# A gated delta rule whose token inverse is taken in 64x64 chunks, in a two-layer diffusion trunk on one core

## The chip, the core and the metric

The kernel runs on one core of one Trainium2 chip. The metric is the device time of one execution in microseconds. TensorE is called PE in the rows (PEld for its weight loads), VectorE DVE, ScalarE ACT, GpSimd POOL, and SyncE, which issues most loads, SP.

## What is computed

Two layers of a trunk over two samples of 128 tokens (prompt and latent), model width 1024. Each layer: modulated norm, one input projection, four groups of heads side by side (gated delta rule, retention, neighbourhood attention, short convolution; 4 heads of 64 each), output projection, and then 32 experts, top 2 of one group. The modulation ("ada") is a product of the conditioning with a 1024 x 6144 matrix, in 8 tiles of 768 columns. Everything is float32. What the change is about is the delta rule, run forwards and on the flipped tokens:

```python
decay = jnp.exp(jnp.where(causal, gc[..., :, None] - gc[..., None, :], -jnp.inf))
kb = k * bt[..., None]
low = jnp.where(strict, jnp.einsum('nbhcd,nbhed->nbhce', kb, k) * decay, 0.0)
t_inv = lax.linalg.triangular_solve(eye + low, jnp.broadcast_to(eye, low.shape), left_side=True, lower=True)
u = t_inv @ (v * bt[..., None])
w = t_inv @ (kb * jnp.exp(gc)[..., None])
attn = jnp.einsum('nbhcd,nbhed->nbhce', q, k) * decay
def step(s, xs):
    qd, at, ui, wi, kd, cd = xs
    v_new = ui - wi @ s
    o = qd @ s + at @ v_new
    s = s * cd[..., None, None] + jnp.einsum('bhcd,bhce->bhde', kd, v_new)
    return s, o
```

The reference takes chunks of 64 tokens; the result does not depend on the size of the chunk.

## The kernel before

Each engine has its own program, written out by hand, and the engines wait for one another by named semaphores (`sem[...]`; `rise(l, name, n)` is the count to wait for in layer l). On TensorE, VectorE, ACT and GpSimd the two layers are one loop (`Fori(0, DEPTH)`, L398, L882, L1136, L1570), so the counts to wait for are computed in registers, and the end of the body branches back. SyncE's program has its two layers written out. At the end of a layer the experts' part stands twice, once for the case that no expert has over 32 tokens, which is the one taken, and once for the other (`pe.If`, `pe.Else`, L802 and L841).

Weights come through a ring of four slots of 3 MB. A load waits until the product that last used its slot is done: 8 ada tiles, 5 pieces of the input projection, 3 of the output projection, 32 experts. The first expert's load waits for ada tile 7, the next three for the pieces of the output projection.

Order of a layer on TensorE: ada tiles 0 to 2 (L414) and the norm's sums (L430); input projection (L454 to L480); attention and retention (L487 to L564), with ada tiles 3 and 4 in between; the delta rule (L569 to L694); output projection (L708); router (L720); experts (L743 gathers tokens, L769 gate and up, L783 down, L792 scatters).

The delta rule treats a sample of 128 tokens as one chunk. For sample s (first 0, then 1) TensorE makes the gates' differences (L578, L579), the products of keys with keys and queries (L586), beta along the rows (L592) and some small ones, VectorE masks and multiplies (L1347 to L1359). Then the inverse of the 128x128 unit triangular matrix of each of 4 heads and 2 directions g is built by doubling, in 7 levels b:

```python
for h in range(HEADS):
    last = mm(ps[:, 2 + g, h * P:(h + 1) * P], group(g, 6)[:, h, :],
              group(g, 3)[:, h, :] if b else ident, start=True, stop=True)   # L633
for h in range(HEADS):
    last = mm(ps[:, 4 + g, h * P:(h + 1) * P], group(g, 4)[:, h, :], group(g, 5)[:, h, :], start=True, stop=True)  # L654
for h in range(HEADS):
    last = mm(ps[:, g, h * P:(h + 1) * P], group(g, 5)[:, h, :], group(g, 4)[:, h, :], start=True, stop=True)      # L658
```

`group(g, 6)` is the level's part of the triangle (GpSimd, L1631), `group(g, 3)` and `group(g, 4)` the inverse so far and its transpose (VectorE adds to them, L1397 and L1399), `group(g, 5)` the first product copied out by ACT (L1046). Level 0 has only L633, level 6 lacks L654. Ada tiles 5 and 6 are cut into pieces between the levels of sample 0, tile 7 stands at the start of sample 1. Then come the products with the values (L671), outputs (L683), for sample 0 the states (L689). After both samples the outputs are normed (ACT L1050, PE L694, ACT L1053 and L1055, DVE L1419 and L1421).

Each float32 product is two instructions in the trace, two loads and two matmuls. Where a product has a `tile_position`, it uses a part of the array: the ada products and gate and up use four tiles of all rows and 32 columns (128*32), the scatter four tiles of 32 rows (32*128).

## Time and profile before

| | us |
|---|---|
| median of 3 runs | 1213.41 (1213.16 to 1215.55) |
| profiled execution, its own time | 1213.35 |
| its span | 1211.7 |
| mean granted TensorE clock | 0.922 of full |

| layer 0, us from the span's start | stage |
|---|---|
| 0 to 42 | ada tiles 0 to 2, first norm |
| 42 to 137 | input projection |
| 137 to 181 | attention, retention |
| 181 to 313 | delta rule |
| 313 to 369 | output projection, second norm, router |
| 369 to 606 | experts |

Layer 1 begins behind 606 and takes the same stages. The span counts from the first to the last instruction of the profiled execution. A busy engine is not an engine that sets the time: what counts is which wait ends last in a stage. "Issue" in a row is time in which an engine waited for nothing that the profile shows.

### The profile page before, as it was taken

The page shows a single profiled execution, that of the slowest core. Times are in us where ns is not written, and L with a number is a line of the kernel's source. Part 1 is how long each engine was busy: PE and PEld are TensorE (multiplying, and loading weights), DVE is VectorE, ACT ScalarE, POOL GpSimd, SP SyncE. Part 2 cuts the span into 40 slices and gives each one's busy share as a digit, 9 for nine tenths or more (in the row PEclk, how much of TensorE's full clock was granted, in tenths as well). Part 3 has the DMA queues.
Part 4 walks back from the last instruction along what each step waited for, and adds up shares of the span by engine and source line. Part 5 has one row for each costly group of instructions (what it writes and reads, how often), then busy time and mean ns, then how long its engine had stood idle before and what let it go on. Part 6 is the DMA issues. An engine that isn't in the chain of part 4 may idle for free.

```text
span 1211.7 us, 28903 instructions
## 1 busy us (share of the span) xinstructions
PE 995.8 (82%) x12852; PEld 828.6 (68%) x12852; DVE 345.9 (29%) x701; ACT 259.3 (21%) x566; POOL 86.6 (7%) x93
## 2 busy tenths in 40 slices
PE   4889868989878897787757998699899698878775
PEld 3489767879766665555544996588888676666653
DVE  0155644354133000000023546443541510000001
ACT  1224431202012111111113353211120221111111
POOL 0000112213000000000000002022320000000000
PEclk9789988999978999999877999799999699999998
DMA  9944631021162999999987355111203459999993
GB/s 387 428 176 170 271 121 39 4 92 51 39 274 111 429 424 430 429 427 428 426 342 294 145 207 219 74 36 36 110 2 148 164 231 426 426 429 428 428 425 167
DMA packets 15668, 299.69 MB, mean 247 GB/s; under 512 B 2224, under 2 KB 2224, under 8 KB 2736
## 3 DMA queue, kind: packets, MB, share of 16 engines
q1 hardware_dynamic: 15120, 296.67, 58.9%
q8 instruction: 108, 1.77, 0.6%
q0 software_dynamic: 416, 1.05, 0.3%
q14 instruction: 24, 0.20, 0.0%
HBM read 295.61 MB, written 2.10 MB: 246 GB/s over the span
## 4 chain that ended last, share of the span: by engine, by line
PE 58%; DMA 24%; issue 7%; DVE 6%; ACT 3%; POOL 1%; SPq 0%; DVEq 0%; POOLq 0%; ACTq 0%
DMA ring<-in_moe 22%; PE ps L769 6%; PE ps L708 5%; PE ps L478 4%; PE ps L633 4%; PE ps L479 4%; PE ps L480 4%; PE ps L658 4%; PE ps L654 3%; PE ps L783 3%; PE ps L454 3%; PE ps L743 3%; DMA ring<-in_ada_w 2%; PE ps L414 2%; PE ps L792 2%
## 5 line engine op out<-in xcount | busy, mean ns | idle before, releaser
L769 PE MATMUL ps<-ring,arena 128*32 128x128 f32 x4096 | 136.1, 285 | 73.4 <-DMA ring<-in_moe 62.4
L769 PEld LDWEIGHTS ps<-ring,arena 128*32 128x32 f32 x4096 | 115.2, 114 | 101.3 <-DMA ring<-in_moe 57.8
L478 PE MATMUL ps<-arena_r 128*128 128x256 f32 x384 | 109.9, 286 | 10.4 <-DVE ring_r L1198 10.4
L1540 DVE COPY arena<-ps 128x128 f32<-128x128 f32 x64 | 18.7, 292 | 339.8 <-PE ps L769 339.8
L480 PE MATMUL ps<-arena_r,ring_r 128*128 128x256 f32 x384 | 108.9, 284 | 0.0
L479 PE MATMUL ps<-hT_r,arena_r 128*128 128x256 f32 x384 | 108.7, 283 | 0.0
L1098 ACT ACTIVATE arena<-ps 128x256 f32<-128x256 f32 x64 | 24.6, 384 | 298.4 <-PE ps L783 298.4
L414 PE MATMUL ps<-ring,condp 128*32 128x128 f32 x1536 | 58.3, 303 | 31.1 <-DMA ring<-in_ada_w 15.4
L478 PEld LDWEIGHTS ps<-arena_r 128*128 128x128 f32 x384 | 73.7, 192 | 10.6 <-DVE ring_r L1198 10.6
L743 PE MATMUL ps<-arena 128*128 128x128 f32 x512 | 75.3, 294 | 3.2 <-DVE arena L1520 3.2
L783 PE MATMUL ps<-ring,arena 128*32 128x256 f32 x1024 | 72.6, 386 | 3.8 <-issue 3.8
L743 PEld LDWEIGHTS ps<-arena 128*128 128x128 f32 x512 | 64.2, 198 | 14.5 <-issue 11.1
L792 PE MATMUL ps<-arena 32*128 32x256 f32 x1024 | 73.3, 400 | 1.0 <-ACT arena L1098 1.0
L479 PEld LDWEIGHTS ps<-hT_r,arena_r 128*128 128x128 f32 x384 | 73.7, 192 | 0.0
L480 PEld LDWEIGHTS ps<-arena_r,ring_r 128*128 128x128 f32 x384 | 73.6, 192 | 0.0
L414 PEld LDWEIGHTS ps<-ring,condp 128*32 128x32 f32 x1536 | 46.5, 122 | 39.0 <-issue 23.8
L1198 DVE TENSOR_TENSOR ring_r<-ring,arena_r 128x2048 fp32r<-128x2048 f32 x24 | 54.8, 2291 | 56.7 <-ACT arena_r L936 56.4
L1631 POOL TENSOR_TENSOR arena<-arena,const 128x512 f32<-128x512 f32 x56 | 60.5, 1094 | 125.5 <-PE ps L633 65.0
L708 PE MATMUL ps<-hT,ring 128*128 128x256 f32 x256 | 59.5, 396 | 5.7 <-DVE hT L1421 5.7
L708 PEld LDWEIGHTS ps<-hT,ring 128*128 128x128 f32 x256 | 50.8, 199 | 14.9 <-DVE hT L1421 7.4
L633 PE MATMUL ps<-arena 128*128 128x128 f32 x384 | 51.8, 290 | 5.9 <-POOL arena L1631 5.8
L633 PEld LDWEIGHTS ps<-arena 128*128 128x128 f32 x384 | 47.9, 202 | 9.3 <-DVE arena L1391 5.2
(278 smaller groups left out, 1357.0 us busy)
## 6 DMA issues: line engine op xcount, KB each, us to landing
ring<-in_moe SPq DMA_DIRECT2D x64, 3072.0 KB, 18.1
ring<-in_ada_w SPq DMA_DIRECT2D x16, 3072.0 KB, 11.4
ring<-in_w_feat SPq DMA_DIRECT2D x8, 3072.0 KB, 17.6
ring<-in_w_tok SPq DMA_DIRECT2D x2, 2112.0 KB, 27.5
ring<-in_w_out SPq DMA_DIRECT2D x2, 2048.0 KB, 7.1
ring<-in_w_out SPq DMA_DIRECT2D x4, 1024.0 KB, 4.8
param<-in_param SPq DMA_DIRECT2D x2, 1442.0 KB, 23.2
xT<-in_xT SPq DMA_DIRECT2D x1, 1024.0 KB, 12.5
```

The source lines that it names most:

```text
L414: last = mm(ps[j:j + 32, bank_in, 0:P], condp[:, k, lead:lead + 32], slot[:, k * 768 + m * P:k * 768 + (m + 1) * P], start=u < 4, stop=u > ...
L478: mm(out, hi, ph_hi[:, k, :], start=k == 0, stop=False)
L479: mm(out, hi, h_lo[:, k, :], start=False, stop=False)
L480: last = mm(out, low[:, k, tile], ph_hi[:, k, :], start=False, stop=k == KT - 1)
L633: last = mm(ps[:, 2 + g, h * P:(h + 1) * P], group(g, 6)[:, h, :], group(g, 3)[:, h, :] if b else ident, start=True, stop=True)
L708: last = mm(ps[:, f // 2, (f % 2) * TOK:(f % 2 + 1) * TOK], slot[:, at:at + P], hT[:, k, :], start=k == 0, stop=k == KT - 1)
L743: last = mm(ps[:, gather_bank(q, k // 2), 256 + (k % 2) * P:256 + (k % 2 + 1) * P], ht[:, s, k * P:(k + 1) * P], sel[:, s, QUAD * q:QUAD * ...
L769: last = mm(ps[32 * j:32 * j + 32, 4, 0:P], xg[:, e // QUAD % 2, k, cols], slot[:, at:at + P], start=k == 0, stop=k == KT - 1, tile_positi ...
L783: last = mm(ps[32 * j:32 * j + 32, 6, 0:256], act_t[:, e % 2, kk * CAP:(kk + 1) * CAP], slot[:, at:at + 256], start=kk == 0, stop=kk == 1, ...
L792: last = mm(ps[:, j, half * TOK:(half + 1) * TOK], ye[rows, e % 2, half * P:(half + 1) * P], spread[rows, e % 2, :], start=False, stop=e = ...
L1198: tt(tiles768(ring_r[in_load(i) % RING][:], cols), tiles768(ring[in_load(i) % RING][:], cols), pw_hi[v % 2], ALU.subtract).then_inc(sem["p ...
L1631: G.tensor_tensor(group(g, 6), group(g, 2), bc(levels[:, g, b, :].unsqueeze(1), HEADS, P), ALU.mult)\
```

## The change

The delta rule's matrices are cut into 64-token chunks, and both samples go together. A group g is now a sample and a direction (4 groups), and holds for 4 heads two 64x64 blocks, one per half of the partitions. `by_chunk` makes 8 products, 4 heads in each of the tiles (0, 0) and (64, 64). The doubling has 6 levels instead of 7, each over 4 groups, `against(n)` (the first product) running two steps ahead of `onto(n)` (the two that extend the inverse and its transpose; in the last level only the transpose). In place of level 6, the values are solved in three thin rounds: the first chunk's, what crosses into the second chunk, and the second chunk's. The gates' differences are made from a row product and a per-partition scalar, with 16 masks on VectorE and the products moved ahead of the retention's variance; keys are multiplied by beta before the key products. Ada tile 5 stands ahead of the key products, tile 6 between the thin rounds, tile 7 behind the states, each whole. The padded copies of keys and queries (POOL L1585 and L1595, ACT L993) and the zeroing of L1614 and L1615 go. The constants get three new blocks (320 columns, ahead of the levels' masks), and the masks shrink. The layer loop is written out on all engines.

```diff
-LEVELS = 7
+LEVELS = 6
+CHUNK = 64
...
+    ("neg_f", P), ("neg_b", P), ("eye", CHUNK),
+    ("levels", 2 * LEVELS * CHUNK))
...
-            with pe.Fori(0, DEPTH) as l:
+            for l in range(DEPTH):
...
+                for g in range(4):
+                    s, d = divmod(g, 2)
+                    for h in range(HEADS):
+                        last = mm(ps[:, 4 + g, h * P:(h + 1) * P], bc(gdec[:, s, d * 4 + h:d * 4 + h + 1], P), upto[d], start=True, stop=True)
+                    last.then_inc(sem["gr_mm"], 1)
...
+                                n, at = d * 4 + 2 * j + i, (2 * j + s) * P
+                                last = mm(ps[part64(i), d, at:at + P], bc(beta[:, s, n:n + 1], CHUNK), ident, start=True, stop=True,
+                                          tile_position=(0, CHUNK * i), skip_group_check=True)
+                    last.then_inc(sem["brow_mm"], 1)
...
+                pe.wait_ge(sem["kd_dve"], rise(l, "kd_dve", 1))
+                ada(ADA_FIRST + 2, 2)
...
+                def by_chunk(out, weights, moving):
+                    for h in range(HEADS):
+                        for c in range(2):
+                            last = mm(out[part64(c), h * CHUNK:(h + 1) * CHUNK], weights[part64(c), h, :], moving(c, h),
+                                      start=True, stop=True, tile_position=(CHUNK * c, CHUNK * c), skip_group_check=True)
+                    return last
...
+                    by_chunk(ps[:, 4 + g % 2, 0:256], low_b[:, g],
+                             (lambda c, h: inv[part64(c), g, h, :]) if b else (lambda c, h: ident[part64(c), part64(c)])).then_inc(sem["inv_dmm"], 1)
...
+                    if b < LEVELS - 1:
+                        by_chunk(ps[:, 2 + g % 2, 0:256], inv_t[:, g], lambda c, h: prod[part64(c), g, h, :])
+                    by_chunk(ps[:, 2 + g % 2, 256:512], prod[:, g], lambda c, h: inv_t[part64(c), g, h, :]).then_inc(sem["inv_umm"], 1)
...
+                for n in range(4 * LEVELS + 2):
+                    if n < 4 * LEVELS:
+                        against(n)
+                    if n > 5:
+                        onto(n - 2)
...
+                    pe.wait_ge(sem["inv_upd"], rise(l, "inv_upd", step(LEVELS - 1, g)))
+                    for h in range(HEADS):
+                        last = mm(ps[part64(c), solve_bank(g), h * CHUNK:(h + 1) * CHUNK], inv_t[part64(c), g, h, :], z[part64(c), g, h, :],
+                                  start=True, stop=True, tile_position=(CHUNK * c, CHUNK * c), skip_group_check=True)
+                    last.then_inc(sem["first_mm"], 1)
+                pe.wait_ge(sem["at_dve"], rise(l, "at_dve", 1))
...
+                pe.wait_ge(sem["off_dve"], rise(l, "off_dve", 1))
...
+                        last = mm(ps[part64(1 - c), solve_bank(g), h * CHUNK:(h + 1) * CHUNK], off[part64(c), s, h, :], vn[part64(c), g, h, :],
+                                  start=True, stop=True, tile_position=(CHUNK * c, CHUNK * (1 - c)), skip_group_check=True)
+                    last.then_inc(sem["cross_mm"], 1)
...
+                ada_transpose(ADA_FIRST + 3, 7)
...
+                last.then_inc(sem["gs_mm"], 1)
+                ada(ADA_FIRST + 4, 6)
...
-            with act.Fori(0, DEPTH) as l:
+            for l in range(DEPTH):
...
+                        act.wait_ge(sem["inv_dmm"], rise(l, "inv_dmm", 4 * b + g + 1))
+                        go(prod[:, g].rearrange("p h c -> p (h c)"), ps[:, 4 + g % 2, 0:256], ACT.Copy).then_inc(sem["inv_dev"], 1)
...
-            with dve.Fori(0, DEPTH) as l:
+            for l in range(DEPTH):
...
+                    for h in range(HEADS):
+                        last = stt(decay[:, g, h, :], ps[:, 4 + g, h * P:(h + 1) * P], ngc[:, 4 * g + h:4 * g + h + 1], neg[g % 2], ALU.add, ALU.add)
+                    last.then_inc(sem["gr_mask"], 1)
...
+                    last = tt(kb[:, d].rearrange("p j s t -> p (j s t)"), A("qkv")[:, 512:1024], bank(d), ALU.mult)
+                last.then_inc(sem["kb_dve"], 1)
...
+                        last = tt(four(low[part64(c), g]), kk, four(decay[part64(c), g, :, part64(c)]), ALU.mult)
...
+                    tt(inv[:, g], ps[:, 4 + g % 2, 0:256].rearrange("p (h c) -> p h c", h=HEADS), eye, ALU.add)
+                    tt(inv_t[:, g], low_b[:, g], eye, ALU.add).then_inc(sem["inv_upd"], 1)
...
+                            t = both[:, g].rearrange("p b h c -> p (b h c)")
+                            tt(t, t, bank(2 + g % 2), ALU.add).then_inc(sem["inv_upd"], 1)
+                        else:
+                            t = inv_t[:, g].rearrange("p h c -> p (h c)")
+                            tt(t, t, ps[:, 2 + g % 2, 256:512], ALU.add).then_inc(sem["inv_upd"], 1)
+                        if b == 1:
+                            last = value(g)
+                            if g % 2 == 1:
...
-            with pool.Fori(0, DEPTH) as l:
+            for l in range(DEPTH):
...
+                        G.tensor_tensor(low_b[:, g], low[:, g], bc(levels[:, g % 2, b, :].unsqueeze(1), HEADS, CHUNK), ALU.mult)\
+                         .then_inc(sem["inv_c"], 1)
```

TensorE in one level of the inverse (ps is PSUM, arena the work space in SBUF). Before, one of two groups:

```order
L627 REGISTER_ALU
L629 REGISTER_ALU [waits inv_c]
L633 MATMUL ps<-arena 128x128 [waits inv_upd]
L633 MATMUL ps<-arena 128x128 x3
...
L650 REGISTER_ALU
L651 REGISTER_ALU [waits inv_dev]
L654 MATMUL ps<-arena 128x128 [waits inv_upd]
L654 MATMUL ps<-arena 128x128 x3
L658 MATMUL ps<-arena 128x128 x4
```

Now, one and a half of four groups, of the steps `against` (8 products) and `onto` (16):

```order
L634 MATMUL ps<-arena 64x64 [waits inv_dev,inv_upd,inv_c]
L634 MATMUL ps<-arena 64x64 x7
L634 MATMUL ps<-arena 64x64 [waits inv_dev,inv_upd]
L634 MATMUL ps<-arena 64x64 x15
L634 MATMUL ps<-arena 64x64 [waits inv_dev,inv_upd,inv_c]
```

The products keep their number per group and shrink from 128x128 to 64x64; the register instructions are gone, the waits stand on the products.

TensorE behind the inverse. Before, for a sample:

```order
L671 MATMUL ps<-arena 128x64 [waits inv_upd]
L671 MATMUL ps<-arena 128x64 x3
L683 MATMUL ps<-arena 128x128 [waits ada_dve,vn_dve]
L683 MATMUL ps<-arena 128x128 x7
L689 MATMUL ps<-arena 128x256 [waits kd_dve]
```

Now, for both samples:

```order
L684 MATMUL ps<-arena 64x64 x3
L404 MATMUL ps<-ring,condp 32x128 [waits slot_in3,at_dve]
L404 MATMUL ps<-ring,condp 32x128 x47
L694 MATMUL ps<-arena 64x64 [waits first_act,off_dve]
...
L412 MATMUL ps<-const,adarow 128x12 [waits ada_row,const_in]
L702 MATMUL ps<-arena 64x64 [waits rest_dve]
...
L714 MATMUL ps<-arena 64x128 [waits qd_dve,vn_dve]
...
L721 MATMUL ps<-arena 64x64 x8
L404 MATMUL ps<-ring,condp 32x128 [waits slot_in0]
L404 MATMUL ps<-ring,condp 32x128 x47
L727 MATMUL ps<-arena,const 128x512 [waits ada_dve,gn_sq]
```

Three thin rounds (L684, L694, L702) with ada tile 6 between, then outputs, states, and ada tile 7 ahead of the norm's product (L727).

TensorE at the end of a layer, the last rows of the case that is not taken (its loop L868, now L901). Before:

```order
L868 COMPARE_AND_BRANCH
L841 UNCONDITIONAL_BRANCH
L398 REGISTER_ALU
L398 COMPARE_AND_BRANCH
L147 UNCONDITIONAL_BRANCH
```

Now, the end of layer 0:

```order
L901 COMPARE_AND_BRANCH
L874 UNCONDITIONAL_BRANCH
L404 MATMUL ps<-ring,condp 32x128 [waits slot_in0,layer_done,cond_silu]
L404 MATMUL ps<-ring,condp 32x128 x47
L419 MATMUL ps<-arena,const 128x256 [waits norm_sq]
```

The branch back at L398 is gone, and layer 1's first ada products stand behind the unused case.

## Rows read from the trace of the kernel before

**Rows 1.** The page: engines' busy time; DMA queue: packets, MB, share
```profile
PE 995.8 (82%) x12852; PEld 828.6 (68%) x12852; DVE 345.9 (29%) x701; ACT 259.3 (21%) x566; POOL 86.6 (7%) x93
q1 hardware_dynamic: 15120, 296.67, 58.9%
```

**Rows 2.** Windows: us, busy PE, PEld, DVE, ACT, POOL, PEclk, DMA share, GB/s
```profile
200.00:240.00 40.00, 38.79 (x383) 35.00 (x384) 19.60 (x30) 6.51 (x12) 14.07 (x13) 0.96 0.08 28
...
345.00:369.00 24.00, 14.33 (x65) 13.07 (x63) 11.67 (x51) 6.98 (x17) 0.00 (x0) 0.63 0.38 150
...
445.00:606.00 161.00, 128.18 (x2586) 95.19 (x2582) 11.08 (x43) 24.75 (x85) 0.00 (x0) 0.97 1.00 427
```

**Rows 3.** The chain of waits: start us, us, what; both layers
```profile
181.44 1.14 PE ps L564 x2
...
309.15 1.14 PE ps L694 x2
...
313.13 22.67 PE ps L708 x96
...
778.97 1.14 PE ps L564 x2
...
910.52 22.67 PE ps L708 x96
```

**Rows 4.** Timeline, one level: start us, us, engine, operation [idle before]
```profile
282.22 1.95 PE L633 MATMUL ps<-arena 128*128 128x128 f32 x16
...
283.32 0.60 ACT L1046 ACTIVATE arena<-ps 128x512 f32<-128x512 f32 x1 [4.00 <-PE ps L633]
...
284.04 1.15 PE L654 MATMUL ps<-arena 128*128 128x128 f32 x8
...
285.23 0.69 DVE L1397 TENSOR_TENSOR arena<-arena,ps 128x512 f32<-128x512 f32 x1 [2.12 <-PE ps L654]
...
287.71 1.95 PE L633 MATMUL ps<-arena 128*128 128x128 f32 x16
```

**Rows 5.** Timeline, products in tiles and thin products
```profile
155.98 2.83 PE L414 MATMUL ps<-ring,condp 128*32 128x128 f32 x96
...
302.44 2.00 PE L671 MATMUL ps<-arena 128*128 128x64 f32 x16
...
374.64 1.96 PE L769 MATMUL ps<-ring,arena 128*32 128x128 f32 x64 [0.55 <-ACT arena L1074]
...
604.06 1.15 PE L792 MATMUL ps<-arena 32*128 32x256 f32 x16 [0.50 <-ACT arena L1098]
```

**Rows 6.** Timeline and page, single costs of the other engines
```profile
265.08 0.42 DVE L1371 TENSOR_TENSOR arena<-ps,egc 128x256 f32<-128x256 f32 x1
...
606.05 4.22 DVE L1428 SCALAR_TENSOR_TENSOR xT<-ps,adaT,xT 128x128 f32<-128x128 f32 x16 [4.58 <-PE ps L792]
...
L1631 POOL TENSOR_TENSOR arena<-arena,const 128x512 f32<-128x512 f32 x56 | 60.5, 1094 | 125.5 <-PE ps L633 65.0
```

**Rows 7.** L398's branch; timeline between the layers; DMA issues of 590:625 us
```profile
L398 PEldq COMPARE_BRANCH  x2: 79/3764/7450, 611.2 to 1205.1; - x2
...
610.30 0.33 SPq L370 DMA_DIRECT2D param<-in_param  x1
...
619.01 5.33 PE L414 MATMUL ps<-ring,condp 128*32 128x128 f32 x93 [13.81 <-issue]
...
629.64 2.29 DVE L1155 TENSOR_TENSOR hT<-xT,rstd 128x2048 f32<-128x2048 f32 x1 [19.36 <-ACT rstd L902]
...
636.17 3.19 ACT L910 ACTIVATE hT<-hT,adaT,scale 128x128 f32<-128x128 f32 x8 [0.90 <-DVE scale L1148]
...
param<-in_param SPq DMA_DIRECT2D x1, 59.5 KB, 16.1
```

**Rows 8.** Timeline: the start, the experts' loads
```profile
32.20 5.26 PE L414 MATMUL ps<-ring,condp 128*32 128x128 f32 x96 [3.55 <-DMA ring<-in_ada_w]
...
267.23 77.57 SPq L328 DMA_DIRECT2D ring<-in_moe  x4
```

591 lines of the change are left out of this document (284 added, 307 removed).

## The prediction

> **What bounds the kernel now.** The page comes first: TensorE is busy for 82% of the span, VectorE for 29%, and the DMA engines for 59% [rows 1]. An average hides where each of them ends the waits, so the windows come next. While the experts' weights stream in, the DMA share is 1.00 at 427 GB/s; in the delta rule (200 to 240 us) it is 0.08 and TensorE is busy for 38.8 of 40 us [rows 2]. The kernel is a chain of stages in which TensorE is the limit, then a stage in which the DMA is, once per layer. The change works in the first kind only.
>
> Then the chain of waits gives the length of what changes. From the retention's variance product (L564) to the first product of the output projection (L708) it takes 313.13 - 181.44 = 131.7 us in layer 0 and 910.52 - 778.97 = 131.6 us in layer 1 [rows 3]. This is over a fifth of the span, twice 131.7 = 263 us. The timeline of one doubling level of the second sample shows what it is made of: L633 starts at 282.22 and again at 287.71, 5.49 us later, and between them stand 48 instructions of 128x128 (L633 x16, then L654 and L658, x8 each, for either group), that is 0.112 us each [rows 4]. ACT (0.60 us) and VectorE (0.69) lie beside it. Counting all levels of both samples, a layer has 72 such groups of 8, 64 us of TensorE.
>
> **The inverse, now.** It has 6 levels, and 4 groups (two samples, two directions) follow one another. A helper, by_chunk, issues 8 products of 64x64, each as 2 instructions: 16 instructions. Calls per layer: 24 in against(), 2 in each of the 16 onto() of the levels 1 to 4, 1 in each of the last 4, together 60 calls in place of the 72 groups. So the price of one call decides. No row shows a product in a 64x64 tile. The nearest rows: four tiles of 128x32 (the ada products) stream 96 instructions in 2.83 us, 0.029 each; and weights of the full width against 64 columns (L671) cost 2.00 / 16 = 0.125 each, the same as wide ones [rows 5]. Half of the columns should load in half the time, 0.056 in place of 0.112, and a call alternates between two tiles on different rows; that loads on different rows overlap is seen in L792 (four tiles of 32 rows, each with weights 128 wide: 1.15 / 16 = 0.072 [rows 5], though a load of that width takes 35.00 / 384 = 0.091 [rows 2]). The bounds are 0.029 and 0.125. I take 0.033, near the first, because its rows are tiled as these are, and a little above it for the two or three waits ahead of each call. A call is 16 x 0.033 = 0.53 us, 60 calls 31.8 us.
>
> Does anything else bound a step? A step (one group of one level) is 3 calls, 1.6 us. VectorE adds 128x512 in 0.69 and then does one piece of other work: 0.42 for 128x256 [rows 6], at most three of these (1.3) for the second sample's values. ACT copies 128x256, half of the 128x512 that take 0.60 [rows 4], and GpSimd multiplies 128x256, half of the 128x512 that take 1.09 [rows 6]. All but those two steps fit; the groups' latencies are covered by the other groups. I add 3.0 us for level 0, where only two groups fit in PSUM and two adds (0.8 us) stand between them. **Inverse: 34.8 us.**
>
> **Before it**, from the moment L564 starts now (its input is ready): VectorE has 16 mask instructions of 128x128, at 4.22 / 16 = 0.26 us together 4.2 us [rows 6]. TensorE does what is left of the gate products (32 instructions from L561's end on, 2.1 us of them still to come), then the variance product (1.1); ACT follows with a logarithm and an exponential (1.25), VectorE with the retention's last two instructions (1.4). They end at 5.9 us. Two 128x256 and two 128x512 follow (kdg, kb): 8.0 us. TensorE meanwhile goes on: ada tile group 5 (2.83 us) runs from 6.6 to 9.4, the key products by chunk 32 instructions x 0.04 = 1.3, and then what needs no answer: 32 + 16 + 8 + 16 instructions and a transpose, some 4.1 us. With the hand-overs **15.3 us** to the first inverse product; VectorE's 8 multiplications of 64x256 (3.0) end inside this.
>
> **After it**: three rounds of thin products (first solve, crossing, second solve), each 32 instructions that stay in one tile for 8 at a time, at half of L633's price, 0.055: 1.8 us each; ada group 6 between the first two (2.83); an answer of ACT or VectorE behind each (0.4 to 0.6); then the outputs (48 x 0.055 = 2.65), copy and square (1.4), ada group 7 (2.83), the norm's product (1.1), two ACT and two VectorE instructions (2.7), as between 309.15 and 313.13 now [rows 3]. With the hand-overs **19.7 us**. Of the ada work nothing is saved: it now stands in the chain, 3 x 2.83 us, but it did before too, in pieces.
>
> Sum: 15.3 + 34.8 + 19.7 = 69.8 us instead of 131.7: 61.9 us less per layer, 123.8 in all.
>
> Here a rule speaks against a term. All loads of L654 are on the same rows as the products before them, and yet 8 of them take 0.112 us each, with 0.11 needed by the product alone [rows 4]: load and product overlap. The Trainium skill, page "TensorE: Matmul & The Clock Gate", Part 3, states that a weight load overlaps products in flight only when their row groups differ. By that rule the 12 groups of thin products would take twice 0.44 us, 5.3 us more per layer, and the sum would end near 1095; the trace disagrees, and I keep 0.055.
>
> **The layer loop.** TensorE's last expert product of layer 0 starts at 604.06 and its next one at 619.01; it sits idle for 13.81 us with no releaser. The loop's line shows why: its branch back starts at 611.2 and takes 7450 ns [rows 7], and the engine had come past the unused case by then, 6 us after its last product. VectorE ends the layer at 610.27 [rows 6]. Written out, the way past the unused branch of the experts stays (until 611.2), the branch back goes: a start 7.7 us earlier. What is late next is the small parameter load: issued at 610.30, 16.1 us to landing, 626.4; VectorE waits for it ahead of L1155, which starts at 629.64 now [rows 7]. Behind it (2.3 us) the last ada columns follow, two rounds of TensorE, VectorE and ACT at some 2.0 us: the modulation starts at 630.7 instead of 636.17, **5.5 us** earlier; the ends are 0 (the next code is fetched as slowly) and 7.7. At the start 320 more columns of constants go ahead of the third ada load, for which TensorE waits at 32.20 [rows 8]: 0.16 MB at 427 GB/s, **+0.4 us**. Register instructions vanish from the queues; where an engine waits anyway they cost nothing, and I count nothing.
>
> **Later stages.** The first expert's load was issued at 267.23 [rows 8] since ada group 7 was early; now it goes some 6 us ahead of the output projection. At 427 GB/s its 3 MB take 7.4 us, and gate and up products of expert 0 start at 374.64 [rows 5], 61 us behind the projection's start: hidden. The other loads hang on the projection and on the experts as before, so the DMA-bound stage keeps its length.
>
> Forecast: the profiled execution took 1213.35 us (span 1211.7), within 0.1 us of the median; 1213.35 - 123.8 - 5.5 + 0.4 = **1084.5 us**.
>
> **Rivals.**
> 1. *Two tiles in turn, not together.* If a call's two tiles do not overlap, an instruction costs 0.055, a call 0.88, the inverse 60 x 0.36 = 21 us more per layer: 1127. Against it: L792 and the ada rows overlap fully. For it: L792's row tiles write four different PSUM banks, by_chunk's two write the same one. The page "TensorEngine Tiling (Array Packing)" of the Trainium skill, Restrictions and Gotchas, states that different row tiles cannot access the same PSUM bank simultaneously; no row here shows such a pair. Chance 0.16.
> 2. *A step waits for answers.* If hand-overs are not covered and a step takes 2.1 us, 20 steps give 10 us more per layer: 1105. Chance 0.13.
> 3. *TensorE's clock.* The granted clock is 0.63 from 345 to 369 us, where TensorE pauses, and 0.96 in the levels [rows 2]. If small tiles count for little and it stays at 1.2 GHz in the inverse, that doubles 32 us per layer: 1148. Against it: 0.97 among the experts' tiles [rows 2]. Chance 0.05.
> 4. *Slower than before.* If an instruction in a 64x64 tile costs what L671's does, 0.125, a call is 2.0 us, the inverse 123 us, the 96 instructions of the thin rounds 7 us dearer, and a layer 15.3 + 123 + 19.7 + 7 = 165 us, 33 more than 131.7: 1213 + 66 - 5 = 1274. It decides from about 0.10 us on: (131.7 + 2.5 - 38) / 960. Chance 0.03.
>
> The forecast itself has 0.60; 0.03 is left for less than the range. The low end is instructions at 0.029 (3.8 us less per layer), 7.7 at the loop and 4 us less per layer elsewhere: 1067. The high end takes in rival 1 with nothing gained at the loop: 1134. A measurement of this kernel tells 0.2%, 2.4 us, from no change. Faster 0.96, within it 0.01, slower 0.03.
>
> **What would show it.** L634: 960 instructions per layer, 16 in some 0.5 us, 35 us from first to last; the chain from L567 to L741 near 70 us; idle before L404 in layer 1 under 7 us, and L1185 waiting for the parameters. I am wrong if L634's x16 take 0.9 us or more, if "issue" ahead of them adds up to over 5 us, or if the experts' stage grows.

## The result, and the profile after

| | before | changed |
|---|---|---|
| median of the runs | 1214.35 us (4 runs, 1213.16 to 1215.55) | 1074.99 us (4 runs, 1072.14 to 1077.56) |
| profiled execution, its own time | 1213.35 | 1072.84 |
| its span | 1211.7 | 1070.9 |
| mean granted TensorE clock | 0.922 | 0.930 |

The ratio is 0.8843, with a 95% interval of 0.8812 to 0.8874. The forecast was 1084.5 us. The changed kernel is 9.5 us faster than that by the medians and 11.7 us by the profiled executions, and lies inside the range of 1067 to 1134.

The page of the changed kernel, the engines' busy time and the DMA queue, answers to [rows 1]:

```profile
PE 880.6 (82%) x13868; PEld 730.0 (68%) x13868; DVE 306.6 (29%) x685; ACT 246.5 (23%) x562; POOL 48.5 (5%) x77
...
q1 hardware_dynamic: 15120, 296.31, 66.6%
```

TensorE has 115 us less to do, with 1016 instructions more, and its share is 82% as before. The gain lies in what a product costs, not in how many there are.

The windows in the delta rule and among the experts (columns as in [rows 2]):

```profile
200.00:240.00 40.00, 38.13 (x1142) 36.81 (x1144) 24.94 (x49) 9.46 (x25) 11.54 (x18) 1.00 0.09 30
...
386.00:547.00 161.00, 121.56 (x2448) 91.36 (x2452) 14.54 (x56) 25.60 (x79) 2.00 (x3) 0.95 1.00 427
```

From 200 to 240 us TensorE issues 1142 instructions where it issued 383, at a granted clock of 1.00. The experts' stretch runs at a DMA share of 1.00 and 427 GB/s in both kernels. From the first product of the output projection to the end of the layer on VectorE it takes 543.8 - 247.2 = 296.6 us now and 610.27 - 313.13 = 297.1 before: that stage has kept its length.

The chain of waits through the delta rule of layer 0 (start us, us, what), which answers to [rows 3]:

```profile
184.17 0.88 PE ps L567 x2
188.49 2.83 PE ps L404 x96
...
192.35 0.46 PE ps L605 x32
...
196.34 0.64 PE ps L634 x16
...
228.77 1.32 PE ps L684 x32
230.09 2.76 PE ps L404 x96
...
247.19 20.99 PE ps L741 x96
```

and its marks in layer 1:

```profile
706.49 0.88 PE ps L567 x2
...
718.67 0.64 PE ps L634 x16
...
750.65 1.32 PE ps L684 x32
```

The variance product is now L567. VectorE's masks (L1368) start when its input is ready, at 182.0 and 704.3 us; this is the point from which the prediction counts. From there to the output projection (L741, at 247.19 and 769.08) it takes 65.2 and 64.8 us, in place of 131.7 and 131.6.

TensorE's timeline has the durations (start us, us, line, shapes, count, [idle before]):

```profile
191.25 1.10 PE L596 MATMUL ps<-arena 64*64 64x128 f32 x32
192.17 0.64 PE L605 MATMUL ps<-arena 64*64 64x64 f32 x32
...
201.00 9.53 PE L634 MATMUL ps<-arena 64*64 64x64 f32 x304 [0.32 <-DVE arena L1429]
210.77 18.00 PE L634 MATMUL ps<-arena 64*64 64x64 f32 x576 [0.24 <-POOL arena L1671]
228.61 1.49 PE L684 MATMUL ps<-arena 64*64 64x64 f32 x32
```

and its windows have the price of an instruction where nothing interrupts the stream (instructions of L634 alone: us, busy PE, PEld, granted clock, DMA share, GB/s):

```profile
217.00:224.00 7.00, 7.00 (x242) 7.00 (x244) 1.00 0.02 5
```

The 576 instructions from 210.77 take 18.00 us, 0.0313 each. Between 217 and 224 us the price is 7.00 / 242 = 0.029; the rest of the 18.00 us is in a few short breaks, the longest 0.34 us, in which no instruction starts. L596 and L605 use four tiles of 64x64: 32 instructions of 128 columns in 1.10 us, and 32 of 64 columns in 0.64. Such a duration ends with the last instruction's own time (0.22 us for L605), which weighs on a short group; in the chain, which goes on with the next product, L605 has 0.46 us, 0.014 each.

Between the layers, the timeline of all engines, which answers to [rows 7]:

```profile
539.57 4.23 DVE L1487 SCALAR_TENSOR_TENSOR xT<-ps,adaT,xT 128x128 f32<-128x128 f32 x16 [4.56 <-PE ps L825]
543.82 0.33 SPq L364 DMA_DIRECT2D param<-in_param  x1
...
545.62 4.91 PE L404 MATMUL ps<-ring,condp 128*32 128x128 f32 x92 [6.88 <-issue]
...
558.27 2.29 DVE L1185 TENSOR_TENSOR hT<-xT,rstd 128x2048 f32<-128x2048 f32 x1 [14.48 <-DMA param<-in_param]
...
562.71 3.18 ACT L943 ACTIVATE hT<-hT,adaT,scale 128x128 f32<-128x128 f32 x8 [0.96 <-DVE scale L1178]
```

The idle time ahead of layer 1's first ada tile is 6.88 us of issue, in place of 13.81. The modulation starts 562.71 - 543.80 = 18.9 us behind layer 0's end; before, it was 636.17 - 610.27 = 25.9.

Where the 140.8 us of span went, from these marks:

| stretch | before | changed | less |
|---|---|---|---|
| start to the output projection, layer 0 | 313.13 | 247.19 | 65.9 |
| to the end of layer 0 (VectorE) | 297.1 | 296.6 | 0.5 |
| to the modulation of layer 1 | 25.9 | 18.9 | 7.0 |
| to the output projection, layer 1 | 274.35 | 206.37 | 68.0 |
| to the end | 301.2 | 301.8 | -0.6 |

### The profile page after: what moved, and what is told of

Read it like the earlier page. It is cut to its first block, busy times and chain, and to the rows that moved or that the text cites. A ratio compares the mean times of both kernels' runs of the same rounds, so it can differ in the third digit from the quotient of the medians.

```text
span 1070.9 us, 30181 instructions
## 1 busy us (share of the span) xinstructions
PE 880.6 (82%) x13868; PEld 730.0 (68%) x13868; DVE 306.6 (29%) x685; ACT 246.5 (23%) x562; POOL 48.5 (5%) x77
## 4 chain that ended last, share of the span: by engine, by line
PE 55%; DMA 31%; DVE 7%; ACT 3%; issue 2%; SPq 0%; POOL 0%; DVEq 0%; POOLq 0%; ACTq 0%
DMA ring<-in_moe 29%; PE ps L802 6%; PE ps L741 5%; PE ps L634 5%; PE ps L467 4%; PE ps L469 4%; PE ps L468 4%; PE ps L404 3%; PE ps L443 3%; PE ps L816 3%; DMA ring<-in_ada_w 3%; PE ps L776 2%; PE ps L825 2%; PE ps L753 1%; DVE xT L1487 1%
## 5 line engine op out<-in xcount | busy, mean ns | idle before, releaser
L802 PE MATMUL ps<-ring,arena 128*32 128x128 f32 x4096 | 133.9, 286 | 77.2 <-DMA ring<-in_moe 76.2
L1599 DVE COPY arena<-ps 128x128 f32<-128x128 f32 x64 | 18.6, 291 | 346.7 <-PE ps L802 346.7
L467 PEld LDWEIGHTS ps<-arena_r 128*128 128x128 f32 x384 | 73.7, 192 | 10.7 <-issue 10.7
L776 PE MATMUL ps<-arena 128*128 128x128 f32 x512 | 76.1, 296 | 3.3 <-DVE arena L1579 3.3
L776 PEld LDWEIGHTS ps<-arena 128*128 128x128 f32 x512 | 65.1, 201 | 15.7 <-issue 15.7
L404 PE MATMUL ps<-ring,condp 128*32 128x128 f32 x1536 | 52.7, 300 | 24.9 <-DMA ring<-in_ada_w 15.8
L816 PE MATMUL ps<-ring,arena 128*32 128x256 f32 x1024 | 69.8, 390 | 0.0
L404 PEld LDWEIGHTS ps<-ring,condp 128*32 128x32 f32 x1536 | 47.9, 121 | 28.6 <-issue 25.9
L741 PE MATMUL ps<-hT,ring 128*128 128x256 f32 x256 | 59.1, 394 | 5.5 <-DVE hT L1480 5.5
L741 PEld LDWEIGHTS ps<-hT,ring 128*128 128x128 f32 x256 | 50.6, 198 | 13.1 <-DVE hT L1480 5.7
L634 PE MATMUL ps<-arena 64*64 64x64 f32 x1792 | 55.6, 219 | 2.1 <-DVE arena L1429 1.3
L634 PEld LDWEIGHTS ps<-arena 64*64 64x64 f32 x1792 | 53.9, 135 | 3.8 <-POOL arena L1671 2.4
L825 PEld LDWEIGHTS ps<-arena 32*128 32x128 f32 x1024 | 46.5, 184 | 11.5 <-ACT arena L1128 2.0
```

The source lines that it names most:

```text
L404: last = mm(ps[j:j + 32, bank_in, at:at + P], condp[:, k, lead:lead + 32], slot[:, k * 768 + m * P:k * 768 + (m + 1) * P], start=u < 4, st ...
L467: mm(out, hi, ph_hi[:, k, :], start=k == 0, stop=False)
L634: last = mm(out[part64(c), h * CHUNK:(h + 1) * CHUNK], weights[part64(c), h, :], moving(c, h), start=True, stop=True, tile_position=(CHUNK ...
L741: last = mm(ps[:, f // 2, (f % 2) * TOK:(f % 2 + 1) * TOK], slot[:, at:at + P], hT[:, k, :], start=k == 0, stop=k == KT - 1)
L776: last = mm(ps[:, gather_bank(q, k // 2), 256 + (k % 2) * P:256 + (k % 2 + 1) * P], ht[:, s, k * P:(k + 1) * P], sel[:, s, QUAD * q:QUAD * ...
L802: last = mm(ps[32 * j:32 * j + 32, 4, 0:P], xg[:, e // QUAD % 2, k, cols], slot[:, at:at + P], start=k == 0, stop=k == KT - 1, tile_positi ...
```

## The experiments

Times are medians; the kernel before took 1214.0 to 1214.8 us in the three sets of runs.

### 1. The layer loop alone

The kernel before, and on each of the four engines:

```diff
-            with pe.Fori(0, DEPTH) as l:
+            for l in range(DEPTH):
```

> The kernel before, with the layer loop written out on the four engines and nothing else changed. The prediction's term for this is 5.5 us less, 1213.4 - 5.5 = 1207.9 us, with the branch of 7450 ns gone between the layers and the modulation 5.5 us earlier behind the end of layer 0, and the rest of the kernel as long as before. In the changed kernel the stretch from layer 0's end to the modulation is 7.0 us shorter (18.9 in place of 25.9). Theory A: that is all due to the loop, so this kernel takes 1206 to 1207 us and shows the same 18.9 us. Rival B: part of the 7.0 us comes from elsewhere, and this kernel gains 4 us or less. Rival C: register instructions ahead of products cost time too, then it gains over 9 us, and the stretch from L564 to L708 shrinks below 131 us.

Measured: 1206.43 us (1205.12 to 1208.1), ratio 0.9933 (0.9913 to 0.9952), 8 us less by the medians and 7.0 by the spans. Its timeline between the layers:

```profile
605.95 4.22 DVE L1428 SCALAR_TENSOR_TENSOR xT<-ps,adaT,xT 128x128 f32<-128x128 f32 x16 [4.21 <-PE ps L792]
...
611.71 3.90 PE L414 MATMUL ps<-ring,condp 128*32 128x128 f32 x82 [6.23 <-issue]
...
631.31 3.18 ACT L910 ACTIVATE hT<-hT,adaT,scale 128x128 f32<-128x128 f32 x8 [0.96 <-DVE scale L1148]
```

Layer 0 ends at 605.95 + 4.22 = 610.17, and the modulation (ACT, L910) starts at 631.31, 21.1 us later, in place of 25.9. The idle time ahead of L414 has fallen to 6.23 us. So 4.8 us lie where the prediction had put 5.5, and the changed kernel has another 2.2 us there. Some of this is scatter between executions: VectorE's wait for the small parameter load lasts 15.35 us here and 14.48 in the first profile of the changed kernel, but 15.33 in its second (run 9), where the modulation starts 19.5 us behind layer 0. Within its first ada tile the changed kernel waits 0.63 us for instructions, this one 2.35, between 82 and 14 of them; what sets such a wait was not tried. Another 1.7 us come up to L564 of layer 1, which starts at 772.43 in place of 778.97: the input projection's first products take 15.70 and 3.64 us (L454, L459) where they took 16.67 and 4.51, at a granted clock of 0.88 in place of 0.76 over the 14 us from the start of the modulation. Whether the shorter wait between the layers gave this clock back no run shows: the changed kernel waits hardly longer and has 0.76 there.

In the delta rule the chain is as long as before, from L564 at 181.98 to L708 at 313.42, 131.4 us: the register instructions ahead of the wide products cost nothing. So theory A is right in the total, and has 4.8 of its 7.0 us in the stretch that it named; rivals B and C fall.

### 2. The order of the two tiles

```diff
                 def by_chunk(out, weights, moving):
-                    for h in range(HEADS):
-                        for c in range(2):
+                    for c in range(2):
+                        for h in range(HEADS):
```

> The changed kernel, with the two loops of by_chunk exchanged: the four products of one 64x64 tile, then the four of the other. Nothing else differs. Theory A (the two tiles run beside each other only when a product of one stands directly behind one of the other): an instruction costs what it does in the thin rounds, whose 32 in one tile at a time take 1.49 us, 0.047 each, in place of 0.031. A call then takes 0.75 us instead of 0.50, the 60 calls 15 us more per layer, and the kernel 30 us more: 1105 us. Rival B (one tile after the other, as the prediction's rival 1 has it, 0.055): 23 us per layer, 1121 us. Rival C (the order does not matter, since queued products of both tiles overlap, or VectorE and not TensorE sets the step): within 5 us of the changed kernel's 1075.

Measured: 1088.61 us (1086.39 to 1089.7). The chain, inverse of layer 0:

```profile
201.44 31.51 PE ps L634 x864
```

An instruction costs 31.51 / 864 = 0.0365 us in place of 0.0313. The inverse, from its first product to the first thin solve, takes 37.1 us in both layers in place of 32.3 and 31.9, 10.0 us more in all; the other 3 to 4 us of the medians are not in this stretch. None of the three theories had the size. The two tiles do work beside each other, and best when their products alternate; but with four of one tile in a row most of the overlap is still there.

The traces of the single instructions say why theory A's price was off. In the changed kernel's first thin round (L684) instructions that follow one another in one tile start 0.058 us apart (228.61, 228.66, 228.72, 228.78, 228.84). Where the tile changes, instructions of the two tiles start in pairs, 0.004 to 0.006 us apart, one pair every 0.058 us. One tile alone costs 0.058, and two beside each other half of that, 0.029. The 0.047 that theory A took for the price of one tile alone, 1.49 / 32, is neither: the round has stretches of both kinds, and its 1.49 us end with the 0.22 us that the last instruction takes by itself (from first to last start it is 1.27 us, 0.041 each). In this run 16 instructions (8 in one tile, 8 in the other) take 16 x 0.0365 = 0.58 us, ten times 0.058: six of these ten starts are pairs.

### 3 and 4. The price of a call, and the PSUM bank

Ahead of the first products of the last two levels:

```diff
+                    if b > 3:
+                        pe.wait_ge(sem["off_dve"], rise(l, "off_dve", 1))
+                        for _ in range(5):
+                            for h in range(HEADS):
+                                for c in range(2):
+                                    mm(ps[part64(c), 0, h * CHUNK:(h + 1) * CHUNK], low_b[part64(c), g, h, :], inv[part64(c), g, h, :],
+                                       start=True, stop=True, tile_position=(CHUNK * c, CHUNK * c), skip_group_check=True)
```

> The changed kernel with 5 further calls of 16 instructions ahead of each of the 8 first products of the last two levels, 640 instructions per layer, both tiles writing the same PSUM bank (0), whose content is not used. It prices a call by itself. Theory A (TensorE sets the pace of the inverse, 0.031 us per instruction): 20.0 us per layer, 40 us in all, 1115 us. Rival B (the step waits for answers of VectorE and ACT, busy for 24 of its 32 us): the further work is partly hidden in those steps, 30 us or less.

The fourth is the same with `ps[part64(c), c, ...]`: each tile has its own bank.

> As the one with 5 further calls per first product of the last two levels, but the two tiles write different PSUM banks (0 and 1) in place of the same one. The page "TensorEngine Tiling (Array Packing)" of the Trainium skill, Restrictions and Gotchas, states that different row tiles cannot access the same bank simultaneously. Theory A (the bank makes no difference; two tiles on different rows and different partitions overlap either way): the same time as with one bank, within 2 us, 0.031 us per instruction. Rival B (sharing the bank costs something): split banks are cheaper, at best 0.0265 per instruction (half of the 0.053 that the thin rounds suggest for a tile by itself), 6 us less in all.

Measured: 1111.93 us (1110.91 to 1113.98) with one bank, 1111.05 (1106.54 to 1113.94) with two. The chain, one group of the further products (L657) in either; one bank:

```profile
226.23 2.27 PE ps L657 x78
```

two banks:

```profile
231.43 2.27 PE ps L657 x78
```

78 instructions take 2.27 us in both, 0.0291 each. The 1280 further instructions make 1280 x 0.0291 = 37.3 us, and the kernel with one bank is 36.9 us above the changed one: nothing of them is hidden. So TensorE sets the pace of the last two levels, and here it makes no difference whether two tiles on different rows write the same bank or two. The page "TensorEngine Tiling (Array Packing)" of the Trainium skill, Restrictions and Gotchas, says that different row tiles cannot access one bank simultaneously; the traces disagree for two tiles that write different partitions of it, since with one bank too an instruction costs 0.0291 us, half of the 0.058 of one tile alone. Two row tiles on the same partitions of a bank were not tried.

### 5. Half of the inverse's products

```diff
                 def by_chunk(out, weights, moving):
-                    for h in range(HEADS):
+                    for h in range(HEADS // 2):
```

> The changed kernel with by_chunk making the products of two heads in place of four, so half of the inverse's products are left out (and its result for two heads is not the inverse); ACT, VectorE and GpSimd work as before. It shows what stands right behind TensorE in the inverse. Theory A (TensorE alone sets it and the others are well covered): 480 of 960 instructions go, 15 us less per layer, the inverse from 32.3 to 17.3 us, the kernel at 1045 us. Rival B (VectorE is next: 24 of the 32.3 us busy, and a wait of an add for the products of its own step): the inverse stops at 24 to 26 us, 7 us less per layer, the kernel at 1061. Rival C (it was answers all along that set the step): no change, 1075.

Measured: 1066.94 us (1063.45 to 1070.41), 8 us less. From L634's first instruction to the thin solve (196.09 to 223.54 in the chain) layer 0's inverse takes 27.5 us in place of 32.4: a third of the 15 us that the left out work took. The timeline of two steps shows the next limit:

```profile
214.90 0.69 DVE L1421 TENSOR_TENSOR arena<-ps,arena 128x512 f32<-128x512 f32 x1
215.09 0.92 PE L634 MATMUL ps<-arena 64*64 64x64 f32 x24 [0.28 <-POOL arena L1671]
215.50 0.68 DVE L1440 TENSOR_TENSOR arena<-arena,ps 128x512 f32<-128x512 f32 x1
216.09 0.69 DVE L1421 TENSOR_TENSOR arena<-ps,arena 128x512 f32<-128x512 f32 x1
...
216.28 0.92 PE L634 MATMUL ps<-arena 64*64 64x64 f32 x24 [0.28 <-POOL arena L1671]
```

and over four such steps (columns as in [rows 2]):

```profile
214.30:219.00 4.70, 3.63 (x100) 3.20 (x98) 4.70 (x9) 1.53 (x4) 2.54 (x4) 1.00 0.01 3
```

VectorE's two instructions of a step (L1440, the add, and L1421, the scores) stand one behind the other, 1.20 us a step, and TensorE's 24 instructions (0.92 us) wait. The rows put TensorE's wait down to GpSimd (L1671), whose product ends last before it; but each such product is wanted only four steps later, and GpSimd is busy for 2.54 of the 4.70 us, VectorE for all 4.70. With all heads a step has 48 instructions, at 0.029 to 0.0313 us each 1.40 to 1.50 us. So TensorE stands 0.2 to 0.3 us per step above VectorE in the steps in which VectorE has its second instruction, and rival B is right in kind; its 24 to 26 us were a little low. The prediction's second rival (a step of 2.1 us) is excluded.

### 6. The thin rounds in alternating tiles

In each of the three rounds, here the first:

```diff
-                for g in range(4):
-                    s, c = divmod(g, 2)
+                for s in range(NS):
...
-                    pe.wait_ge(sem["inv_upd"], rise(l, "inv_upd", step(LEVELS - 1, g)))
+                    pe.wait_ge(sem["inv_upd"], rise(l, "inv_upd", step(LEVELS - 1, 2 * s + 1)))
                     for h in range(HEADS):
+                        for c in range(2):
+                            g = 2 * s + c
```

> The changed kernel with the three thin rounds in pairs of groups: a product of one tile directly followed by one of the other, as in by_chunk, in place of four in one tile. The waits of a pair then stand ahead of its first product. Theory A: a round's 32 instructions take 32 x 0.031 = 1.0 us instead of 1.49, but the answers start later (a pair ends 0.5 us in, its two answers run one behind the other), so of the 1.5 us per layer at most 1.0 shows: 1 to 2 us less, 1073 to 1074. Rival B (a round is bound by its hand-overs, not by its products): no change within 0.5 us, or slower by up to 1 us.

Measured: 1075.0 us (1067.82 to 1077.97), the changed kernel's time. Its timeline:

```profile
228.34 0.63 PE L684 MATMUL ps<-arena 64*64 64x64 f32 x16
229.19 0.68 PE L684 MATMUL ps<-arena 64*64 64x64 f32 x16 [0.22 <-DVE arena L1448]
...
233.17 1.15 PE L696 MATMUL ps<-arena 64*64 64x64 f32 x32
...
237.59 1.53 PE L719 MATMUL ps<-arena 128*64 128x128 f32 x24 [1.21 <-DVE arena L1475]
```

The second round (L696) has shrunk to 1.15 us from 1.54. The first is split by a wait, and the outputs (L719) start 9.25 us behind the first solve in place of 237.22 - 228.61 = 8.61. What the products give, the hand-overs take back: rival B. (Its ratio is 0.8834, 0.8807 to 0.8862; the changed kernel's is 0.8843.)

### 7 and 8. Ada tile 5 out of the chain

```diff
                 ada(ADA_FIRST + 1, 3)
+                ada(ADA_FIRST + 2, 3, 128)
+                ada_transpose(ADA_FIRST + 1, 4)
...
                 pe.wait_ge(sem["kd_dve"], rise(l, "kd_dve", 1))
-                ada(ADA_FIRST + 2, 2)
```

with its copies on ACT and VectorE moved to match.

> The changed kernel with ada tile 5 moved from the chain ahead of the key products to just behind ada tile 4, into the 5.4 us in which TensorE waits for the attention's VectorE and ACT work ahead of L520; its load was issued early enough. Theory A (the prediction's reading that each ada tile in the delta rule stands in the chain with its 2.83 us, and that the wait ahead of L520 does not depend on it): 2.8 us less per layer, 5.6 in all, 1069.5. Rival B (VectorE's masks, kdg and kb set the moment at which the key products start, and the tile only fills that wait): they could start at 189.5 in place of 191.3, 1.5 us less per layer or nothing, 1072 to 1075.

The eighth kernel adds the sixth's edit.

> The changed kernel with ada tile 5 early and the thin rounds in alternating tiles together. If both gains are real and lie in different waits they add: 5.6 + 1.5 = 7 us less, 1068. If VectorE sets the start of the key products and the thin rounds are bound by hand-overs: 0 to 3 us less.

Measured: 1068.0 us (1064.3 to 1069.11), ratio 0.8788 (0.8766 to 0.8809), and with both 1071.72 (1066.65 to 1073.48), ratio 0.8808 (0.878 to 0.8835). The timeline of tile 5 early, where the key products (L597) start:

```profile
185.00 1.27 DVE L1385 TENSOR_TENSOR arena<-arena,ps 128x512 f32<-128x512 f32 x2
186.33 1.10 PE L597 MATMUL ps<-arena 64*64 64x128 f32 x32 [1.96 <-DVE arena L1385]
```

They start 186.33 - 180.65 = 5.7 us behind the variance product, in place of 191.25 - 184.00 = 7.25. So of the tile's 2.83 us the move is worth 1.6 per layer, and then TensorE waits 1.96 us for VectorE's multiplication by beta (L1385): rival B as to the place. Yet the kernel gained some 7 us and not 3. The rest lies ahead of L571: from the attention's L522 to L571 it takes 14.98 us in layer 0, where the changed kernel has 184.00 - 166.15 = 17.85; in layer 1 it takes 17.39, where the changed kernel has 17.78. Twice 1.6, 2.9 and 0.4 make 6.5 us. That led to the next two.

The two edits together are not faster than tile 5 alone, and with overlapping intervals the two kernels can't be told apart. Nothing speaks for the sum of 7 us from two gains; the thin rounds gave nothing in run 6 either.

### 9 and 10. The wait ahead of L520, and the clock

> The changed kernel itself, so that the next two stand against it on the same chip: 1072 to 1077 us, as in the runs of the result. Its profile tells how far the stretch behind the delta rule (L741, 96 instructions, 20.99 us in layer 0 and 24.00 in layer 1 of the first profile) moves with TensorE's granted clock alone.

The tenth issues ada tile 4's products twice, and nothing moves:

```diff
-                    for u in range(ADA_UNITS):
+                    for u in [u for _ in range(times) for u in range(ADA_UNITS)]:
...
-                ada(ADA_FIRST + 1, 3)
+                ada(ADA_FIRST + 1, 3, times=2)
```

> The changed kernel with the products of ada tile 4 issued twice, the second time over the first with the same values: 96 instructions more per layer in the 5.4 us in which TensorE waits ahead of L520, nothing else moved. In the profile of the changed kernel the clock is at half from 166 to 174 us, behind that wait; with ada tile 5 in it, it stayed at full in layer 0 and fell for 7 us later in layer 1. Theory A (the wait itself costs the clock, and work in it holds the clock up): L520's 12 instructions take 1.5 us in place of 2.83, L533's 24 some 3 in place of 4.8, 1.3 to 3 us less per layer, 2.6 to 6 us less in all, though work is added. Rival B (what ada tile 5 gained came from its move alone): the same time as the changed kernel, with L520 at 2.8 us.

Measured: the changed kernel 1075.22 us (1072.76 to 1076.41), ratio 0.8856 (0.8833 to 0.888); with the tile issued twice 1069.68 (1066.89 to 1071.04), ratio 0.8805 (0.878 to 0.883). With 192 instructions more it is 5.5 us faster. TensorE's timeline of the changed kernel again, layer 0:

```profile
157.99 2.83 PE L404 MATMUL ps<-ring,condp 128*32 128x128 f32 x96
166.24 2.82 PE L520 MATMUL ps<-const,arena 128*128 128x128 f32 x12 [5.42 <-DVE arena L1325]
...
170.60 2.07 PE L533 MATMUL ps<-arena 128*128 128x128 f32 x8 [1.30 <-ACT arena L1049]
```

and of the tenth kernel, layer 1:

```profile
681.98 5.45 PE L404 MATMUL ps<-ring,condp 128*32 128x128 f32 x192
690.23 1.53 PE L520 MATMUL ps<-const,arena 128*128 128x128 f32 x12 [2.81 <-DVE arena L1325]
...
693.30 1.16 PE L533 MATMUL ps<-arena 128*128 128x128 f32 x8 [1.41 <-ACT arena L1049]
```

but in its layer 0:

```profile
165.22 1.56 PE L520 MATMUL ps<-const,arena 128*128 128x128 f32 x12 [2.81 <-DVE arena L1325]
...
168.32 2.07 PE L533 MATMUL ps<-arena 128*128 128x128 f32 x8 [1.30 <-ACT arena L1049]
```

with its windows (the number behind POOL's count is the granted clock), of layer 0 and of layer 1:

```profile
168.00:173.00 5.00, 4.68 (x22) 4.68 (x23) 1.79 (x5) 0.27 (x1) 0.00 (x0) 0.50 0.16 69
690.00:704.00 14.00, 12.36 (x96) 11.58 (x97) 8.65 (x20) 2.05 (x2) 0.56 (x1) 1.00 0.30 126
```

L520's 12 instructions take 1.53 and 1.56 us behind a wait of 2.81, and 2.82 behind one of 5.42. This is no accident of one execution: in all seven traces that keep the long wait (5.20 to 5.43 us; the changed kernel twice and runs 2 to 6) they take 2.82 us in both layers. The changed kernel's windows behind that wait, and of two starts of the output projection (the first profile):

```profile
166.00:174.00 8.00, 6.54 (x30) 6.44 (x31) 4.73 (x10) 1.45 (x1) 0.00 (x0) 0.50 0.16 66
247.00:252.00 5.00, 4.80 (x22) 4.26 (x23) 0.14 (x1) 0.00 (x0) 0.00 (x0) 1.00 0.98 421
769.00:774.00 5.00, 4.92 (x12) 3.94 (x13) 0.02 (x1) 0.00 (x0) 0.00 (x0) 0.50 0.94 403
```

The clock is granted at 0.50 (the 1.2 GHz level) for the 8 us behind the long wait. With the wait half filled it held through layer 1's stretch (690.23 to 704.92, 14.7 us for L520 to L567 in place of 17.8) and fell later in layer 0's (168 to 173 us, 17.1 us). So the fill is worth up to 3 us a layer, not each time: in layer 0 the stretch is 0.7 us shorter, and behind the inverse the clock fell again (0.61 from 234 to 238 us), so that L714's 48 instructions take 4.49 us in place of 2.84 and layer 0 keeps nothing. The two profiled executions differ by 2.9 us in span, the medians by 5.5; where the other 2.6 us lie no trace shows. Theory A holds for what stands right behind the wait (L520 in both layers, its 1.3 to 3 us in layer 1); its sum of 2.6 to 6 us fits the medians. Rival B is excluded, since nothing was moved here. The Trainium skill, page "TensorE: Matmul & The Clock Gate", Part 1, says that the clock has two levels and that an idle stretch brings the lower one back; these rows agree. The second profile also gives what run 9 was for: L741's 96 instructions take 22.41 us in layer 0 and 24.02 in layer 1, where the first profile has 20.99 and 24.00.

### 11. All three ada tiles

Tile 6 follows tile 5 into the wait ahead of L520, and tile 7 is cut into three:

```diff
+                ada(ADA_FIRST + 3, 3, 256)
...
-                ada(ADA_FIRST + 3, 6)
+                ada(ADA_FIRST + 4, 6, units=range(0, 16))
...
-                ada(ADA_FIRST + 4, 6)
+                ada(ADA_FIRST + 4, 6, units=range(16, 32))
                 pe.wait_ge(sem["gn_sq"], rise(l, "gn_sq", 1))
                 mm(bank(7), C("blockones"), gn_a, start=True, stop=True).then_inc(sem["gn_mm"], 1)
+                ada(ADA_FIRST + 4, 6, units=range(32, ADA_UNITS))
```

> The changed kernel with ada tiles 5 and 6 both in the wait ahead of L520, and tile 7 in three pieces of 32 instructions: behind the first thin solve, behind the states, and between the norm's product and the output projection. A sum from the profile: L520 starts 0.3 us later, tile 6 leaves the chain (2.8 us), and of tile 7's 2.8 and the 2.7 us of waiting ahead of L741 one 0.9 goes, with 0.5 us exposed ahead of the norm's product. That is 2.5 to 3.5 us per layer beyond the kernel with tile 5 early (1068): 1062 us. Rival B (the clock or the waits of the thin rounds take it back, since TensorE then pauses there): 1066 to 1069.

Measured: 1064.57 us (1061.67 to 1075.47), ratio 0.8779 (0.874 to 0.8818), 10.7 us less than the changed kernel beside it. Its timeline behind the inverse:

```profile
226.68 1.49 PE L688 MATMUL ps<-arena 64*64 64x64 f32 x32
228.10 0.81 PEld L405 LDWEIGHTS ps<-ring,condp 128*32 128x32 f32 x32
...
237.75 0.30 PEld L729 LDWEIGHTS ps<-arena,const 128*128 128x128 f32 x2 [0.25 <-ACT arena L1085]
...
241.74 4.40 PEld L743 LDWEIGHTS ps<-hT,ring 128*128 128x128 f32 x21 [2.12 <-DVE hT L1485]
```

From the first thin solve to the output projection it takes 241.74 - 226.68 = 15.1 us, in both layers, in place of 18.6: 3.5 us per layer as summed. In layer 0 L526 starts at 168.24, 11.5 us behind the start of ada tile 4 (156.71), where the changed kernel has 166.15 - 157.90 = 8.25; 0.3 us later was expected. Behind its 288 ada instructions, which end at 166.7, stand two products with the copied rows (ACT, 166.72 and 167.60), and L526 is queued behind these. The two tiles together are too long for the wait, by 3.3 us. With the wait so full the clock held in layer 0 (L526 took 1.51 us), and yet in layer 1 it took 2.80, as behind the long wait. The time lies between the 1062 us of the sum and the 1066 of rival B: the sum was right behind the inverse and wrong ahead of L526. It has the lowest median, 3.4 us below tile 5 alone, but against the kernel before the ratios are 0.8779 and 0.8788, and the runs don't tell the two apart.

## Why the prediction was right, and where its sizes were off

The mechanism was as written: halved columns, two tiles beside each other, TensorE as the limit of the inverse, the experts' stage unchanged, the loop's branch gone. The forecast took 128.9 us off, and the span fell by 140.8: 11.9 us more. Nearly all terms erred to the same side, so no error hid another.

- **Before the inverse, 15.3 us.** Measured: 182.0 to 196.3, 14.3. The ada tile started 6.5 us in, as summed (6.6). The key products took 1.10 / 32 = 0.034 us per instruction, in place of 0.04, and the 32 of 64 columns behind them 0.64 us (by the chain, where the next product cuts off the last one's own time, 1.03 and 0.46 us).
- **The inverse, 34.8 us.** Measured 32.3 and 31.9. The term that was mis-sized is the price of an instruction, 0.033 by choice between 0.029 and 0.125. It is 0.0313 over the steady steps, breaks included, and 0.0291 where nothing breaks in (217 to 224 us, and the further products of run 3). The row that the price was compared with was read a little low: 5.49 / 48 is 0.114, not 0.112, which changes no term. Level 0 takes 4.7 us for 64 instructions (196.27 to 201.00); the sum had 5.1.
- **After the inverse, 19.7 us.** Measured 18.6. A thin round takes 1.49 to 1.54 us in place of 1.8. The half of L633's price, 0.055, was nearly right for one tile alone (0.058); what the sum left out is that where a group ends and the next one takes the other tile, the two overlap.
- **Weight loads on the same rows.** The rule of the Trainium skill that the prediction cites ("TensorE: Matmul & The Clock Gate", Part 3), that loads overlap products only when row groups differ, would have made the thin rounds dearer than 0.055, with the sum near 1095. They are cheaper, and within one tile, on the same rows, 0.058. Full products say the same more clearly: with only 16 moving columns an instruction costs 3.64 / 32 = 0.114 us (L448), which is then the price of its load; with 256 columns 20.99 / 96 = 0.219 (L741), so the product alone would need some 0.11 for 128 columns, an estimate from that row. Load and product one after the other would be 0.22; [rows 4] has 0.114. The trace disagrees with the rule for these products.
- **Sum per layer, 61.9 us less.** Measured 131.7 - 65.2 = 66.5 and 131.6 - 64.8 = 66.8; the three terms above make the 4.6 and 4.9 by which this is more. In layer 1 another 1.3 us came in the input projection (L443 and L448, 16.21 and 3.64 us, in place of 16.67 and 4.51), at a granted clock of 0.84 in place of 0.81 over its first 14 us.
- **The loop, 5.5 us.** Measured 7.0 in the changed kernel, of which run 1 shows 4.8 by the loop alone. The bound of 7.7 held. The parameters were late next, as the sum had it: VectorE waits for them, 14.48 us up to L1185. The sum had 16.1 us to their landing, as in the one row of before; here it is 14.4, and in the other kernels with the loop written out 13.0 to 16.1 (run 1: 15.2). That load's scatter is the 1.5 us by which the term was too small.
- **The constants, +0.4.** Ada tile 2's wait ended at 32.83 in place of 32.20: +0.6.
- **The experts' stage, nothing.** 0.5 us less in layer 0, 0.6 more in layer 1. The first expert's load left at 243.34, 3.85 us ahead of the projection (6 was written), and stayed hidden.
- **Rival 1** (tiles in turn) is excluded by 0.0313 per instruction, where a tile alone has 0.058; its bank rule was tested in runs 3 and 4. The 0.072 for L792, on which the case against it rested, was read too high: 16 instructions are few, and their 1.15 us end with the last one's own time. In the trace they start 0.051 us apart, a quarter of the 0.21 to 0.22 of a full product of 256 columns. **Rival 2** is excluded, with the margin known (run 5). **Rival 3**: the clock was granted at 1.00 through the inverse. **Rival 4** is excluded by the same price. The chance of 0.16 for rival 1 rested on an unseen pair of tiles; no row of before had two tiles of 64 rows, and only the run could tell.

What the prediction did not see is beside its sum: TensorE's clock in the attention of the changed kernel, and that the ada tiles, of which it wrote that nothing is saved, could stand outside the chain (runs 7 and 11).

## What to carry to other kernels

Where a product fills half of the array's rows and columns, two such products alternating between tiles (0, 0) and (64, 64) cost 0.03 us per instruction here, against 0.058 in one such tile and 0.11 for a full one, and their order is worth 0.005. Price such a call by itself with copies into unused PSUM, and halve it to find what stands right behind it: here VectorE, 5 us away. Look for the waits of the engine that sets the time, and put its independent work there: it leaves the chain, and it can keep the clock up. Put in no more than the wait holds: with two tiles in it L526 came 3.3 us later.

## What the runs showed of the hardware that was not expected

- More work made the kernel faster: 192 instructions in two waits, 5.5 us less (run 10). After an idle stretch of 5.42 us TensorE ran at 0.50 for 8 us. With the stretch half filled, the clock held in one layer and fell 3 us later in the other.
- The same 96 instructions of L741 behind the same 2.74 us of waiting took 20.99 us in layer 0 and 24.00 in layer 1 of one execution; the granted clock was 1.00 from 247 us and 0.50 from 769 us. This alone moves a run by 3 us, more than the 0.2% that a comparison was to tell.
- 64x64 tiles, per instruction of 64 columns: one tile alone 0.058 us, two in turn 0.029, four 0.014. That is two and four tiles at work in the time of one.
- Two tiles on different rows that write one PSUM bank, in different partitions, cost what they do in two banks: 2.27 us for 78 instructions (runs 3 and 4).
